# Four changes of step order in a two-block transformer kernel, and one pipeline for the fourteen groups of heads of its first block

## The reference

```
# first block, one layer
mod = silu(c) @ w_mod + b_mod                      # six shifts, scales and gates
h = rms(x) * (1 + sc1) + sh1
qa,ka,va, qi,ki,wi, qb,kb,vb, qc,kc,vc = split(h @ w_in)
oa = attention of 4 heads over the 128 keys that an index score selects (top-k of relu(qi.ki) weighted by wi)
ob = stick-breaking attention of 4 heads (a cumulative sum of log-sigmoids in place of a softmax)
oc = attention of 8 heads in a window of 128 keys, with sinks
x = x + g1 * (rms_heads([oa, ob, oc]) @ w_o)
x = x + g2 * ((silu(h2 @ w_gate) * (h2 @ w_up)) @ w_down)      # h2 = rms(x) * (1 + sc2) + sh2
# second block, one layer: other attentions and a scan, then
x = x + g_f * rms((relu(h2 @ w_up)**2) @ w_down)
# the rotary tables of the second block are cos and sin of positions * frequencies
```

## Time and profile before

| | us |
|---|---|
| median of 3 runs | 3231.54 |
| lowest and highest of them | 3217.03, 3239.86 |
| the profiled execution, its own time | 3235.96 |
| its span in the trace | 3234.2 |
| TensorE busy in the span | 3009.4 |
| VectorE busy | 1803.9 |
| ScalarE busy | 773.2 |
| GpSimd busy | 931.8 |

### The profile page before, as it was taken

One profiled execution on the slowest core, in us unless ns is written; L12 is line 12 of the kernel. 1 busy time (PEld: TensorE's weight loads), 2 busy tenths in 40 slices (PEclk: granted clock), 3 DMA queues, 4 the chain that ended last, 5 costly groups with the idle time before them and its releaser, 6 DMA issues.

```text
span 3234.2 us, 34034 instructions
## 1 busy us (share of the span) xinstructions
PE 3009.4 (93%) x12282; PEld 2164.4 (67%) x12282; DVE 1803.9 (56%) x3823; ACT 773.2 (24%) x1801; POOL 931.8 (29%) x802
## 2 busy tenths in 40 slices
PE   7988999999899799999989998899998998899997
PEld 3445578888644567888754355788884345688886
DVE  1484359568438646947952634787924444551333
ACT  2244320000124442000022244210112235420111
POOL 0220124443312013444420301344440210243442
PEclk9997899999999799999989989999999998899998
DMA  5105125335211002434421101154421110122221
GB/s 219 71 27 183 52 87 184 107 131 179 105 52 53 27 27 91 172 128 143 147 88 55 52 27 61 65 200 158 169 105 48 35 52 27 53 79 81 101 79 53
DMA packets 39223, 304.93 MB, mean 94 GB/s; under 512 B 4352, under 2 KB 4480, under 8 KB 24848
## 3 DMA queue, kind: packets, MB, share of 16 engines
q1 hardware_dynamic: 39024, 302.68, 25.9%
q0 software_dynamic: 32, 0.07, 0.0%
HBM read 300.63 MB, written 2.10 MB: 94 GB/s over the span
## 4 chain that ended last, share of the span: by engine, by line
PE 71%; DVE 16%; ACT 5%; issue 3%; DMA 3%; POOL 1%; DVEq 0%; SPq 0%; ACTq 0%; POOLq 0%
PE bank L1077 37%; PE bank L1057 9%; PE bank L1405 7%; PE bank L1131 3%; PE bank L1223 3%; DVE nw L2033 3%; DMA ring<-in_slabs 2%; DVE sel L2272 1%; DVE m L2271 1%; PE bank L1538 1%; PE bank L1273 1%; DVE SPT L2336 1%; ACT SPT L1725 1%; PE bank L1260 1%; PE bank L1188 1%
## 5 line engine op out<-in xcount | busy, mean ns | idle before, releaser
L962 POOL TENSOR_TENSOR SPT<-ring 128x512 f32<-128x512 f32 (+2 forms) x140 | 175.6, 1254 | 964.7 <-DMA ring<-in_slabs 503.4
L1077 PE MATMUL bank<-U,ring 128*128 128x256 f32 x1728 | 409.6, 382 | 12.6 <-DVE U L2067 10.7
L1077 PEld LDWEIGHTS bank<-U,ring 128*128 128x128 f32 x1728 | 330.3, 191 | 60.2 <-DVE U L2067 12.3
L2033 DVE SCALAR_TENSOR_TENSOR nw<-sel,c,nw 128x256 f32<-128x256 f32 x504 | 329.5, 654 | 37.6 <-DMA sel<-in_mod_pieces 19.9
L1077 PE MATMUL bank<-U,SPT 128*128 128x256 f32 x1296 | 313.1, 381 | 5.3 <-POOL SPT L967 5.3
L1077 PEld LDWEIGHTS bank<-U,SPT 128*128 128x128 f32 x1296 | 247.4, 191 | 40.9 <-POOL SPT L967 6.9
L1405 PE MATMUL bank<-hT,ring 128*128 128x512 f32 x544 | 252.6, 609 | 6.8 <-ACT hT L1842 6.8
L1077 PE MATMUL bank<-hT,SPT 128*128 128x256 f32 x1088 | 257.0, 379 | 0.0
L1223 PE MATMUL bank<-hT,ring 128*128 128x512 f32 x512 | 242.8, 617 | 4.7 <-ACT hT L1621 4.7
L1077 PE MATMUL bank<-hT,ring 128*128 128x256 f32 x1088 | 246.0, 379 | 0.0
L2093 DVE TENSOR_TENSOR rb<-bank,nw 128x256 f32<-128x256 f32 x108 | 45.6, 422 | 354.2 <-PE bank L1077 257.4
(11 more groups left out here) (343 smaller groups left out, 4658.7 us busy)
## 6 DMA issues: line engine op xcount, KB each, us to landing
ring<-in_slabs SPq DMA_DIRECT2D x88, 2048.0 KB, 8.3
sel<-in_mod_pieces SPq DMA_DIRECT2D x144, 512.0 KB, 4.7
ring<-in_slabs SPq DMA_DIRECT2D x8, 1536.0 KB, 6.7
ring<-in_slabs SPq DMA_DIRECT2D x8, 1280.0 KB, 8.9
ring<-in_slabs SPq DMA_DIRECT2D x2, 2080.0 KB, 8.5
ring<-in_slabs SPq DMA_DIRECT2D x2, 1808.0 KB, 9.2
ring<-in_slabs SPq DMA_DIRECT2D x2, 1664.0 KB, 7.6
cst<-in_consts SPq DMA_DIRECT2D x1, 2112.0 KB, 14.6
```

The source lines that it names most:

```text
L962: pool.tensor_tensor(e1, a21, a22, ALU.add).then_inc(*pool_order.up())
L1077: mm = pe.matmul(into[j][:, c:c + HALF], lhs[:, k, :], rhs[:, k, :], start=(begin and k == 0), stop=(end and k == kp - 1))
L2033: ins = dve.scalar_tensor_tensor(a, w[:, k, :], c[:, j:j + 1], a, ALU.mult, ALU.add)
```

## The change

- In `ffn_steps`, `turn` comes ahead of the `ma`, `ma`, `mt` of its unit, in both blocks; `mm` and `mb` come one unit later.
- The six `idx` steps, which stood together behind tile 5 (counted in the order of projection), are laid between the parts of tiles 5, 6 and 7.
- `angles` becomes three steps behind units 13, 15 and 17 of the first block's last feed-forward part and a step `sine` behind unit 19; its scratch moves from `sqb` to `yB`; the table load behind the sine is gone.
- `group_slots` is called once for all fourteen groups. Its first sixteen chunks (slots 0 to 7) are woven with the projections, the other eighteen with the stick-breaking heads. Before, the eight "c" groups had 22 chunks of their own beside the projections, with an end of the pipeline there, and the six "a" groups 18 of their own.
- `("wo", 0, n)` starts at 0.35 in place of 0.1 of the second stretch in layer 1.

```
@@ -307,6 +307,7 @@
     return out
 
 
+ANGLES_AT = {13: [("angles", 0)], 15: [("angles", 1)], 17: [("angles", 2)], 19: [("sine",)]}
 PIECE_AT1, PIECE_AT2 = tuple(range(1, 12)) + tuple(range(20, 33)), tuple(range(1, 25))
 
 
@@ -314,20 +315,20 @@
 
     o, turn, at = [], 0, None
     for t, u in enumerate(units):
-        if when and t == when[-1] + 2:
+        if when and t == when[-1] + 3:
             o.append(("mb", at))
         o.append(("unit",) + u)
         turn += closes(u)
         if t + 2 < len(units):
             o.append(("S",) + units[t + 2])
+        if u[0] == "gu" and u[2] == wide - 1:
+            o.append(("turn", u[1]))
         if t in when:
             p = when.index(t)
             o += [("ma", 2 * p), ("ma", 2 * p + 1), ("mt", p)]
-        if when and t == when[-1] + 1:
+        if when and t == when[-1] + 2:
             at = 4 * ((turn + 1) % 2)
             o.append(("mm", at))
-        if u[0] == "gu" and u[2] == wide - 1:
-            o.append(("turn", u[1]))
         o += after(t)
     return o
 
@@ -353,26 +354,26 @@
     for m in range(8):
         if (l, m) == (0, 2):
             o.append(("tables",))
-        o += [st for part in tile(m) for st in part]
+        for q, part in enumerate(tile(m)):
+            o += part + ([("idx", m - 4, q // 2)] if m >= 5 and q % 2 else [])
         if m == 3:
             o += [("projv", i) for i in range(QT)]
-        if m == 5:
-            o += [("idx", i, hp) for i in range(1, QT) for hp in range(2)]
         if m >= 6:
             o += [st for chunk_ in rounds[:6] for st in chunk_]
             rounds = rounds[6:]
+    slots = group_slots(range(len(GROUPS1)))
     dense = []
     for m in range(8, 18):
         dense += tile(m)
-    o += woven((-0.03, 0.92, dense), (0.37, 1.01, group_slots(range(NC1))),
+    o += woven((-0.03, 0.92, dense), (0.37, 1.01, slots[:2 * NC1]),
                (0, 1.15, rounds + [[("seldone", i)] for i in range(1, QT)]))
     mods = []
     if l == 0:
         for s in range(MOD_FIRST, MOD_SLABS):
             mods += [[("mg", s)], [("mp", s)]]
         mods.append([("modb",)])
-    o += woven((0, 0.96, stick_slots()), (0.08, 0.95, group_slots(range(NC1, len(GROUPS1)))),
-               (0, 0.55, mods), (0.55 if l == 0 else 0.1, 1, [[("wo", 0, n)] for n in range(KT)]))
+    o += woven((0, 0.96, stick_slots()), (0.08, 0.95, slots[2 * NC1:]),
+               (0, 0.55, mods), (0.55 if l == 0 else 0.35, 1, [[("wo", 0, n)] for n in range(KT)]))
     for n in range(KT):
         o += [("wo", 1, n, 0), ("xq", n, 0)] + ([("xa", n - 1, 0)] if n > 1 else [])
     o += [("S",) + FFN1[0], ("S",) + FFN1[1]]
@@ -387,7 +388,7 @@
     def between(t):
         u = FFN1[t - 1] if t else FFN1[0]
         o = [("xs", 2 * u[2]), ("xs", 2 * u[2] + 1)] if u[0] == "dn" and u[1] == 1 and u[3] == 1 else []
-        return o + ([("angles",)] if (l, t) == (DEPTH - 1, len(FFN1) - 3) else [])
+        return o + (ANGLES_AT.get(t, []) if l == DEPTH - 1 else [])
 
     o += ffn_steps(FFN1, 2, PIECE_AT1, between)
     o += [("xs", KT - 2), ("xs", KT - 1)]
@@ -1778,10 +1779,9 @@
                         k = st[1]
                         act.wait_ge(*s1["xd"].after(l, k // 2 + 1))
                         act.activation(hT[:, k, :], xT[:, k, :], ACT.Square).then_inc(*s1["xs"].up())
-                    elif kind == "angles":
+                    elif kind == "sine":
                         act.wait_ge(pos_ready, 1)
                         act.activation(tab[64:96, :, :], tab[64:96, :, :], ACT.Sin).then_inc(pos_ready, 1)
-                        act.preload_act_table_set("natural_log_exp_and_others")
             for l in range(DEPTH):
                 act.preload_act_table_set("natural_log_exp_and_others")
                 act.sem_clear(act_order.sem)
@@ -2177,12 +2177,14 @@
                     elif kind == "tn":
                         turn_first(l, s1)
                     elif kind == "angles":
-                        dve.wait_ge(pos_in, 16)
                         rows = slice(64, 96)
-                        pf, turns, ang = sqb[rows, 0, :], sqb[rows, 1, :], yB[rows, 0, :]
-                        link(dve.tensor_copy(pf, posi[rows, :]))
-                        link(dve.tensor_scalar(ang, pf, cst[rows, C_MISC + 4:C_MISC + 5], None, ALU.mult))
-                        for t, quarter in ((0, 0.25), (1, 0.0)):
+                        pf, turns, ang = [yB[rows, j, :] for j in range(3)]
+                        if st[1] == 0:
+                            dve.wait_ge(pos_in, 16)
+                            link(dve.tensor_copy(pf, posi[rows, :]))
+                            link(dve.tensor_scalar(ang, pf, cst[rows, C_MISC + 4:C_MISC + 5], None, ALU.mult))
+                        else:
+                            t, quarter = ((0, 0.25), (1, 0.0))[st[1] - 1]
                             a = tab[rows, t, :]
                             link(dve.tensor_scalar(turns, ang, 1.0 / TWO_PI, quarter, ALU.mult, ALU.add))
                             link(dve.tensor_scalar(turns, turns, ROUND, None, ALU.add))
@@ -2194,7 +2196,8 @@
                             ins = dve.tensor_scalar(a, a, -PI_MAX, None, ALU.max)
                             if t == 0:
                                 link(ins)
-                        ins.then_inc(pos_ready, 1)
+                            else:
+                                ins.then_inc(pos_ready, 1)
                     elif kind == "unit" and closes(st[1:]):
                         u = st[1:]
                         if u[0] == "gu":
```

## The result

The changed kernel takes 3260.1 us (median of 6 runs, 3254.0 to 3262.2) against 3232.6 for the kernel before (6 runs): a ratio of 1.0083, with a 95% interval of 1.0069 to 1.0098. I had forecast 3229, with a range that ended at 3258. The profiled execution took 3260.27 with a span of 3258.5, so 24.3 more than the one before.

A forecast was written before the change was run, and what follows sets the result against it. TensorE was taken as the bound (71% of the chain), with VectorE almost as full. Terms -8 - 11 - 13 - 4 + 20 + 14 + 0 = -2 on a 3231.5 median gave 3229 us, range 3188 to 3258.

The forecast's parts named there:

- the waits on the turn: First block's first down units: 10.7 us of TensorE waits go, with 2.3 of slow matmuls behind them, gain 13.
- slab requests: First block's feed-forward parts: turn ahead of `ma` delays each request by 1.9; 16 slabs at 1.25 cost 20 us.
- the second block: Its layer 0, feed-forward: turn waits 1.43 for ScalarE with VectorE nearly full; cost 14 us, bounds 0 and 37.
- the clock's sign in the feed-forward parts: First block's down units: slow matmuls behind removed turn waits booked as 2.3 us gained; none booked behind new slab waits.
- the one pipeline: Attention parts of both layers: removes idle TensorE at the joins, gain 6 plus 5, 11 us; bounds 0 and 17.
- My rival at 3240: Attention: the drain leaves the projections but its idle time returns between the stick-breaking steps; 3229 + 11 = 3240, chance 0.11.
- Idx: Projections, both layers: spreading the steps removes 4.0 us of waits for ScalarE's relu each; gain 8.0, between 4 and 11.
- angles: First block's last feed-forward part: moving the eighteen operations earlier shortens a 4.58 us wait for GpSimd's sums of squares; gain 4.2.
- mm: Feed-forward: fold one unit later removes a 2.87 us wait, but TensorE then waits for the same slab; gain 0, at most 3 a layer.
- VectorE becomes the bound: Rival: every wait for ScalarE and delayed request reaches TensorE whole, 37 + 30 against gains of 36; 3262 us, chance 0.10.
- Slab delay absorbed: Rival: slack at the other slabs absorbs the later requests, so costs are 0; 3231.5 - 36 = 3196 us, chance 0.22.
- the clock stays up: Rival: two low-clock stretches at the end of the projections run at full clock; 3229 - 13 = 3216 us, chance 0.12.

The follow-up runs named there:

- The profile with 375.6: Kernel before with only the queue condition changed, so slabs go ahead of their pieces, turn behind `ma` in both blocks: 3227.0 us, ratio 1.0002.

## Why the prediction was wrong, point by point

**The idle time of the feed-forward parts was forecast about right.** My terms were -10.7 for the waits on the turn, +20 for slab requests and +14 for the second block, together +23.3; measured, +23.2. The terms one by one: the waits for the turn went (-4.9 and -5.5 in the two layers, by the run with both turns back); slab waits of layer 0 grew by 10.7 (forecast 10 a layer); G0's idle time grew by 12.5 against 14. The sizes inside them were less right than their sums: a turn ahead delays the request by 2.9, not by 1.9, because its operations slow down beside GpSimd more than the `ma` gain. The wait for ScalarE is 1.82, not 1.43. And of the 20.2 us of slab waits in layer 0, 7.6 stand before slabs of down units (5.24 and 2.31), where I had counted on one such slab; I had also taken, 220 us long, for the whole supply of such waits before. That sum and measurement meet within 0.1 is luck: four profiles with the old order of these parts and two or three with the new one give on average 27 us more of idle time and 14 more of busy time, 41 together as in the pair above.

**The step that failed is the clock's sign in the feed-forward parts.** I booked slow matmuls only where a wait was removed, as a gain of 2.3, and let the new waits cost their own length. The new waits are followed by slow matmuls as well: +4.9, +5.1 and +7.6 of busy time, 17.6 in all (14 by the averages), so an error of 16 to 20 us. One row of the changed kernel's timeline, layer 0, against another of the same twelve matmuls:

```profile
810.79 5.41 PE L1078 MATMUL bank<-U,ring 128*128 128x256 f32 x12 [5.24 <-DMA ring<-in_slabs]
831.03 2.86 PE L1078 MATMUL bank<-U,ring 128*128 128x256 f32 x12 [2.31 <-DMA ring<-in_slabs]
```

The granted clock from 809.6 to 834.6 was 0.87, so part of it passed at the 1.2 GHz level. My own argument about and the earlier trace rows had this in it, and I used it on one side only. The Trainium skill, TensorE: Matmul & The Clock Gate, section "HAM oscillation — how this bites in real kernels", describes a matmul loop that waits some 3 to 5 us for each slab and starts each time at the low clock. I had cited it only for the denser join, and the slab waits that I forecast, 1.5 to 2, are shorter than the ones it tells of. The row of 5.24 agrees with it; the last section shows low clock behind a shorter wait, too.

**The second step that failed is the one pipeline, 11 us, and with it the later `("wo", 0, n)`, which I put at nothing.** The two together added 0.2, 1.9 and 2.8 us of idle time in the two layers, by three pairs of runs. The later start alone accounts for 4.8 of idle time in layer 1; the pipeline alone, at equal start, saves 0 to 3. So the bound "0 (the idle time comes back one slot later)" is about what happened to the pipeline. My rival at 3240 named this and gave 11 us for it. I had read the waits that the pipeline removes and not asked what stands behind its first slot in ScalarE's queue (4.22, twice) nor that the second head's 5.51 would grow by the steps put ahead of it; I had forecast it a tenth shorter.

**Idx, angles, mm: right.** Idx: 8.0 forecast, 7.7 of idle time measured; the time fell by 13 to 16, the rest being clock in A0; that passes my bound of 11, which allowed the clock too little. How much of this clock part the idx steps bring is not shown, as A0 has run at 375.6 without them. Angles: the wait of 4.58 in the earlier trace rows is gone, and the part with it is 4 to 8 us shorter in every run that has the edit; its eighteen operations cost nothing where they went (F1 at 375.2 like F0). `mm`: nothing, as forecast, for the reason forecast, that the slab behind it was late anyway.

**The rivals.** "VectorE becomes the bound", 3262 with a chance of 0.10, gave nearly the measured time for partly other reasons: it put every delay on TensorE whole, 67 in place of 34, where the measured delays were about my 34, the clock took another 18, and my gains came in smaller. That its number fits is no proof of it. "Slab delay absorbed" is out by the 20.2 us of slab waits (its 3196 also dropped the 14 of the second block, which its reason doesn't touch; it should have been 3209), and "the clock stays up" by the busy time of A0 and A1, 383.6 and 356.2 against 386.1 and 355.8.

**The sum by parts.** Against my -2: 20 from the clock in the feed-forward parts, 9 from A1 (forecast -9, measured 0; about 5 of it is the 0.35), 3 from A0 (forecast -10, measured -7), less 3 each from the closing sum and the earlier start. That makes 26, which is 24.3 + 2.

**Still open.** What decides A0's busy time. Programs with the one pipeline had 372 to 388 there and those without 374 to 387, so the pipeline alone does not decide it. The two profiles of the kernel before agree within 1.3, but chance between executions isn't ruled out: the eleven runs of that one kernel that were timed beside the last four experiments fall into two groups (those beside the others spread over the same range without a clear gap), seven between 3221.5 and 3227.8 us and four between 3233.4 and 3237.6, and both of its profiles (3236.0 and 3233.0) belong with the longer ones. The profile with 375.6 is of an execution of 3224.3, in a kernel whose own runs go from 3217.7 to 3236.1. A gap of about 10 us is just what A0 differs by. No profile of a short execution of the kernel before was taken, so this stays open.

## What to carry to other kernels

In a kernel that TensorE bounds, price each new wait of TensorE at its length and at the slow matmuls behind it; here this was a half to three quarters more again (14 on 27 by the averages, 17.6 on 23.2 in the one pair). Price filler work that is moved as well: the later start of eight projection steps, put at nothing, cost 4.8 us of idle time. Before moving work about between two events on an engine, find the queue that ties a transfer to that engine's progress: here one condition in SyncE's queue turned the change's loss of 27 us into a gain of 45, by letting slabs go ahead of pieces that wait for VectorE. Edits that alone are worth little or cost something (early slabs, a later fold, an earlier turn) were worth 36 to 39 us together in two layers, because each alone only uncovers the next wait.

## What the runs showed of the hardware that I had not expected

Low clock follows short waits too, and not all of them. Two waits of the changed kernel's layer 0 (a third, of 2.37, stands above between them), each before the same eight matmuls:

```profile
489.38 1.99 PE L1078 MATMUL bank<-VT,SPT 128*128 128x256 f32 x8 [2.02 <-POOL SPT L968]
...
543.17 3.54 PE L1078 MATMUL bank<-VT,SPT 128*128 128x256 f32 x8 [2.38 <-POOL SPT L968]
```

Behind 2.02 and 2.37 they ran at full clock, and behind 2.38 most of them did not. And the same order of instructions in A0 had a busy time of 375.6 in one profile and 386.1 in another, of two programs, at idle times of 34.9 and 35.5: the clock alone moved a stage of 400 us by 10.
